# Four raw weight buffers in both expert layers, with the residual input kept outside meanwhile

## The reference

```python
x = x + merged @ w_out[l]
h2 = rmsnorm(x, norm2_g[l])
x = x + peer(h2, ...)           # below
return rmsnorm(x, final_g)
...
# peer, for each token and each of 8 heads: 16 experts out of 128 x 128
s1, s2 = scores of the two halves of the query against 128 keys each
v1, i1 = lax.top_k(s1, PEER_TOPK); v2, i2 = lax.top_k(s2, PEER_TOPK)
vals, flat = lax.top_k(v1 + v2 over all pairs, PEER_TOPK)
gates = jax.nn.softmax(vals, axis=-1)
hid = jax.nn.gelu(jnp.einsum('cd,chkd->chk', xc, u_tab[ec]))
return jnp.einsum('chk,chkd->cd', gc * hid, v_tab[ec])
```

## Time and profile before

| | us |
|---|---|
| runs | 2459.35, 2459.76, 2462.13 |
| median | 2459.76 |
| the profiled execution, its time | 2455.19 |
| its span, first to last instruction | 2453.5 |
| mean granted TensorE clock | 0.988 |
| first unit of the first expert layer starts | 962.8 |
| first unit of the second expert layer starts | 1725.5 |

### The profile page before, as it was taken

One profiled execution on the slowest core, in us unless ns is written; L12 is line 12 of the kernel. 1 busy time (PEld: TensorE's weight loads), 2 busy tenths in 40 slices (PEclk: granted clock), 3 DMA queues, 4 the chain that ended last, 5 costly groups with the idle time before them and its releaser, 6 DMA issues.

```text
span 2453.5 us, 33787 instructions
## 1 busy us (share of the span) xinstructions
PE 2359.6 (96%) x12326; PEld 2047.5 (83%) x12326; DVE 1642.7 (67%) x2048; ACT 1168.2 (48%) x1072; POOL 516.4 (21%) x348
## 2 busy tenths in 40 slices
PE   7999999999999999989989999999999999999997
PEld 6888888888878889988878899999788888888885
DVE  5545766555645555898898888784577666667674
ACT  5534555444444344565556455564443334333342
POOL 0012322000000001222222546453221021211210
PEclk9999999999999999999999999999999999999998
DMA  7755556444466545555555678777898787887871
GB/s 281 267 198 202 215 204 220 151 148 168 141 240 221 217 187 188 194 206 210 210 184 207 255 295 300 286 290 257 338 360 313 267 313 298 306 306 309 317 273 74
DMA packets 91231, 589.99 MB, mean 240 GB/s; under 512 B 10912, under 2 KB 11168, under 8 KB 28944
## 3 DMA queue, kind: packets, MB, share of 16 engines
q1 hardware_dynamic: 58464, 423.65, 47.2%
q0 software_dynamic: 21744, 123.09, 13.6%
q10 hardware_dynamic: 10944, 42.18, 4.3%
HBM read 543.79 MB, written 44.04 MB: 240 GB/s over the span
## 4 chain that ended last, share of the span: by engine, by line
PE 65%; DVE 16%; DMA 9%; issue 6%; ACT 4%; DVEq 0%; SPq 0%; ACTq 0%; POOL 0%; POOLq 0%
PE psum L1196 10%; PE psum L1198 9%; PE psum L1197 9%; PE psum L840 9%; PE psum L842 9%; PE psum L841 9%; DMA w_raw<-in_w_units 8%; DVE w_lo L1250 6%; ACT w_hi L487 3%; DVE hot2a L1596 3%; DVE hot1a L1592 1%; PE psum L974 1%; PE psum L1146 1%; DVE pre_ring L1639 1%; PE psum L1099 1%
## 5 line engine op out<-in xcount | busy, mean ns | idle before, releaser
L1250 DVE TENSOR_TENSOR w_lo<-w_raw,w_hi 128x2048 fp32r<-128x2048 f32 x276 | 637.7, 2317 | 338.9 <-ACT w_hi L487 334.8
L487 ACT ACTIVATE w_hi<-w_raw 128x2048 fp32r<-128x2048 f32 x276 | 527.8, 1914 | 574.8 <-DMA w_raw<-in_w_units 527.6
L1146 PE MATMUL psum<-h2T,w_hi 128*128 128x448 f32 x2048 | 648.8, 375 | 25.7 <-DVE w_lo L1250 16.9
L1147 PE MATMUL psum<-h2T,w_lo 128*128 128x224 f32 x2048 | 544.0, 266 | 0.0
L1146 PEld LDWEIGHTS psum<-h2T,w_hi 128*128 128x128 f32 x2048 | 384.6, 188 | 60.8 <-issue 29.1
L1196 PE MATMUL psum<-w_hi,w_up 128*128 128x512 f32 x1024 | 401.5, 392 | 9.7 <-ACT hs L769 5.2
L1197 PE MATMUL psum<-w_lo,w_up 128*128 128x512 f32 x1024 | 400.3, 391 | 0.0
L1198 PE MATMUL psum<-w_hi,w_low 128*128 128x512 f32 x1024 | 400.3, 391 | 0.0
L1147 PEld LDWEIGHTS psum<-h2T,w_lo 128*128 128x128 f32 x2048 | 391.0, 191 | 0.0
L840 PE MATMUL psum<-w_hi,hT_hi 128*128 128x512 f32 x768 | 306.2, 399 | 12.5 <-DVE w_lo L1250 12.5
L842 PE MATMUL psum<-w_hi,hT_lo 128*128 128x512 f32 x768 | 300.5, 391 | 0.0
(11 more groups left out here) (325 smaller groups left out, 2897.3 us busy)
## 6 DMA issues: line engine op xcount, KB each, us to landing
w_raw<-in_w_units SPq DMA_DIRECT2D x338, 1024.0 KB, 4.9
raw_x<-in_w_units SPq DMA_DIRECT2D x62, 1024.0 KB, 7.6
hid_scratch<-hst ACTq DMA_DIRECT2D x32, 448.0 KB, 2.8
tab_scratch<-gate_a ACTq DMA_DIRECT2D x14, 1024.0 KB, 5.3
h_in<-hid_scratch POOLq DMA_DIRECT2D x16, 896.0 KB, 9.3
g_tab<-tab_scratch POOLq DMA_DIRECT2D x16, 896.0 KB, 14.4
proj_scratch<-evac ACTq DMA_DIRECT2D x24, 512.0 KB, 5.2
x_nat<-in_x POOLq DMA_DIRECT2D x2, 2048.0 KB, 8.7
```

The costliest lines, as they stand in the source:

```text
L487: act.activation(w_hi[:, s % SPLIT, :], w_raw[:, s % RAW, :], ACT.Copy).then_inc(hi_done, 1)
L1146: pe.matmul(psum[:, k % 4, 0:2 * NU].rearrange("p (a t) -> p a t", a=2), uh, h2T[:, c, :, G:S], start=c == 0, stop=False, skip_group_check ...
L1147: ins = pe.matmul(psum[:, k % 4, NU:2 * NU], ul, h2T[:, c, 0, G:S], start=False, stop=c == KC - 1, skip_group_check=True)
L1250: dve.tensor_tensor(w_lo[:, s % SPLIT, :], w_raw[:, s % RAW, :], w_hi[:, s % SPLIT, :].bitcast(F32), ALU.subtract).then_inc(lo_done, 1)
```

## The change

From unit U0 on there are four raw buffers: the two of `w_raw` and two of `raw_x`, which now lie in the place of `x_nat`. For that x leaves the core. POOL writes `x_nat` to a DRAM scratch `x1` as soon as its last block is added, `x_rep` is filled from there, and POOL reads it back into a new tile `x_end` (in the former place of `raw_x`) in the second layer, when the last hidden store has landed. The end of the kernel works on `x_end`. In the second layer the gathered rows are used at other steps: none at k = 1 and 3 of iteration 0, one each at k = 5 and 7, then k = 1, 3 and 5 as before, with the step (5, 1) left out instead of (4, 5).

```diff
-        region(AT_MIX + 16 * KB, AT_MIX + 32 * KB, ("raw_x", [P, 2, UW]))
+        region(AT_X, END, ("raw_x", [P, 2, UW]))
+        region(AT_MIX + 16 * KB, AT_MIX + 32 * KB, ("x_end", [P, NT, D]))
...
-            with sp.Fori(1, (V0 + XR) // RAW) as i:
+            with sp.Fori(1, U0 // RAW) as i:
...
-                sp.wait_ge(hi_done, V0 + XR + s - RAW + 1)
-                sp.wait_ge(lo_done, V0 + XR + s - RAW + 1)
-                sp.dma_start(w_raw[:, s, :], io["w_units"][V0 + XR + s]).then_inc(w_in_s[s], 16)
-            sp.wait_ge(hid_st[0], 16 * U_IT)
-            sp.wait_ge(hid_st[1], 16 * U_IT)
-            sp.wait_ge(gidx_done, 1)
+                sp.wait_ge(hi_done, U0 + s - RAW + 1)
+                sp.wait_ge(lo_done, U0 + s - RAW + 1)
+                sp.dma_start(w_raw[:, s, :], io["w_units"][U0 + s]).then_inc(w_in_s[s], 16)
+            sp.wait_ge(x1_spilled, 16)
+            sp.wait_ge(sq2, 8)
+            sp.wait_ge(xg2_done, 4)
             for s in range(2):
-                sp.dma_start(raw_x[:, s, :], io["w_units"][V0 + XR + 2 + s]).then_inc(w_in_x[s], 16)
-            with sp.Fori(1, (PEER_NK - XR) // XR) as i:
+                sp.dma_start(raw_x[:, s, :], io["w_units"][U0 + 2 + s]).then_inc(w_in_x[s], 16)
+            with sp.Fori(1, (UNITS - U0) // XR) as i:
                 for s in range(XR):
-                    sp.wait_ge(hi_done, i * XR + (V0 + s + 1))
-                    sp.wait_ge(lo_done, i * XR + (V0 + s + 1))
+                    sp.wait_ge(hi_done, i * XR + (U0 + s - XR + 1))
+                    sp.wait_ge(lo_done, i * XR + (U0 + s - XR + 1))
...
+            pool.wait_ge(x1_done, 4)
+            pool.dma_start(x1, x_nat[:, :, :]).then_inc(x1_spilled, 16)
             pool.wait_ge(xt_done, 4)
...
-            pool.wait_ge(x1_done, 4)
+            pool.wait_ge(x1_spilled, 16)
             pool.wait_ge(sc_done, 2)
...
-                pool.dma_start(x_rep[g * G:(g + 1) * G, :], x_nat[0:G, 0, :]).then_inc(rep_in, 16)
+                pool.dma_start(x_rep[g * G:(g + 1) * G, :], x1[0:G, 0, :]).then_inc(rep_in, 16)
...
+            pool.wait_ge(hid_st[0], 16 * U_IT)
+            pool.wait_ge(hid_st[1], 16 * U_IT)
+            pool.wait_ge(gidx_done, 1)
+            pool.dma_start(x_end[:, :, :], x1).then_inc(x1_back, 16)
...
-                    m = 3 * i + k // 2
-                    if k in (1, 3, 5) and m != GJ - PRE:
-                        n = PRE + m - (m > GJ - PRE)
-                        if n < 2 * GJ:
-                            gathered(n)
+                    if (i, k) in row_slots:
+                        gathered(row_slots[i, k])
...
+            open_slots = [(0, 5), (0, 7)] + [(i, k) for i in range(1, U_IT) for k in (1, 3, 5) if (i, k) != (5, 1)]
+            row_slots = dict(zip(open_slots, range(PRE, 2 * GJ)))
...
+            dve.wait_ge(x1_back, 16)
```

More of the change, by code:

```diff
@@ L180, in hybrid_block @@
         x_rep, y_acc, ring, pre_ring, raw_x = buf["x_rep"], buf["y_acc"], buf["ring"], buf["pre_ring"], buf["raw_x"]
+        x_end = buf["x_end"]
         sel = buf["rs_diag"][:, 0, :]
@@ L481, in hi @@
             def hi(n, s):
+                if isinstance(n, int) and n >= U0:
+                    return hi_wide(n, s)
                 act.wait_ge(w_in_s[s % RAW], (n - s % RAW) * (16 // RAW) + 16)
@@ L487, in hi, with hi_wide @@
                 act.activation(w_hi[:, s % SPLIT, :], w_raw[:, s % RAW, :], ACT.Copy).then_inc(hi_done, 1)
-            def hi_second(i, s):
-                if isinstance(i, int) and i == 0 and s < XR:
-                    return hi(V0 + s, s)
-                slot, turn = s % XR, i * 2 + (s // XR - 1)
+            def hi_wide(n, s):
+                slot = s % XR
                 if slot < 2:
-                    act.wait_ge(w_in_s[slot], turn * 16 + 16 * ((V0 + XR) // RAW + 1))
-                else:
-                    act.wait_ge(w_in_x[slot - 2], turn * 16 + 16)
-                act.wait_ge(unit_done, i * 8 + (V0 + s - (SPLIT - 1)))
-                src = w_raw[:, slot, :] if slot < 2 else raw_x[:, slot - 2, :]
+                    src = w_raw[:, slot, :]
+                    act.wait_ge(w_in_s[slot], (n - (U0 + slot)) * (16 // XR) + 16 * (U0 // RAW + 1))
+                else:
+                    src = raw_x[:, slot - 2, :]
+                    act.wait_ge(w_in_x[slot - 2], (n - (U0 + slot)) * (16 // XR) + 16)
+                act.wait_ge(unit_done, n - (SPLIT - 1))
                 act.activation(w_hi[:, s % SPLIT, :], src, ACT.Copy).then_inc(hi_done, 1)
@@ L817, in _ @@
                 act.wait_ge(x2_done, t + 1)
-                act.activation(sq_last[:, :], x_nat[:, t, :], ACT.Square, accum_out=stat[:, t:t + 1]).then_inc(fsq, 1)
+                act.activation(sq_last[:, :], x_end[:, t, :], ACT.Square, accum_out=stat[:, t:t + 1]).then_inc(fsq, 1)
                 act.wait_ge(fms, t + 1)
@@ L1244, in lo @@
             def lo(n, s):
+                if isinstance(n, int) and n >= U0:
+                    return lo_wide(n, s)
                 dve.wait_ge(hi_done, n + 1)
@@ L1729, in _ @@
             dve.wait_ge(gf_in, 16)
+            dve.wait_ge(x1_back, 16)
             for t in range(NT):
                 dve.wait_ge(acc_done, t + 1)
-                dve.tensor_tensor(x_nat[:, t, :], x_nat[:, t, :], psum[:, 4 * t:4 * t + 4, :].rearrange("p b n -> p (b n)"), ALU.add).then_inc(x2_done, 1)
+                dve.tensor_tensor(x_end[:, t, :], x_end[:, t, :], psum[:, 4 * t:4 * t + 4, :].rearrange("p b n -> p (b n)"), ALU.add).then_inc(x2_done, 1)
                 dve.wait_ge(fsq, t + 1)
@@ L1737, in _ @@
                 step(refine(stat[:, 6 + t:7 + t], stat[:, 2 + t:3 + t], 1))
-                dve.scalar_tensor_tensor(out_t[:, t, :], x_nat[:, t, :], stat[:, 6 + t:7 + t], gf[:, :], ALU.mult, ALU.mult).then_inc(out_done, 1)
+                dve.scalar_tensor_tensor(out_t[:, t, :], x_end[:, t, :], stat[:, 6 + t:7 + t], gf[:, :], ALU.mult, ALU.mult).then_inc(out_done, 1)
 ROUND = float(3 << 22)
```

20 lines of the change are left out of this document (10 added, 10 removed).

## The result

| | before | after |
|---|---|---|
| median us | 2458.15 (10 runs, 2455.97 to 2462.50) | 2465.09 (10 runs, 2460.77 to 2468.91) |
| span of the profiled execution | 2453.5 | 2459.3 |

The ratio is 1.0024 (95% interval 1.0014 to 1.0035): the changed kernel is **slower by 0.24%, some 6 us**, where 20 us less were forecast.

What follows compares the result with a forecast made beforehand. TensorE was taken as the bound, with idle or low-clock losses in four places, and VectorE in the first layer's iterations 0 to 7. Terms: -7.9 - 20.5 - 1.6 - 4.0 + 0.6 + 13 = -20.4 us, giving 2439.4, range 2420 to 2464.

Steps and rivals of the forecast that it cites:

- Part 1: First layer, iterations 0 to 7: four raw buffers remove VectorE's waits for w_hi and nothing else, -7.9 us.
- My last sentence: Forecast wrong if TensorE still waits for hot2a, or something unseen in the waits held VectorE's w_lo in iterations 0 to 7.
- Part 2: First layer, iterations 8 to 13: TensorE becomes the bound, idle and clock losses go, -20.5 us, between -10 and -21.7.
- iterations 14 and 15: End of the first layer: the time that TensorE misses there goes, -1.6 us.
- Part 3: Start of second layer: stall at the hs copy goes, but iteration 1's g_tab lands late; -4.0 us, between -8.3 and 0.
- only iteration 1 inherits the late start: +0.6: Second layer, iterations 1 to 4: same slack as before, so just the first of them loses, 0.6 us.
- Part 4: Second layer, iterations 5 to 14: moved rows delay operand loads, an iteration takes 32.4 + L; +13 us, between 0 and +41.
- L: Second layer: g_tab's time from issue to landing, taken as 12.5 us; under 11.1 an iteration takes 43.5.
- The port rule: Second layer: VectorE would hold every gather at the moved rows 2 us more, making the sum -0.4, not -20.4.
- the first term: First layer, iterations 0 to 7: the -7.9 us for VectorE's waits for w_hi.
- (b): Rival, slower: operand load decides the second layer, 49.0 us an iteration, +55 there; +22 in all, 2481; chance 0.14.

Runs made afterwards that it cites:

- half_raw: The kernel after, with only half of each raw weight unit loaded from the first layer's fifth unit on: 2437.69 us, ratio 0.9904 to the kernel before.
- no_skip: The kernel after, with step 1 of iteration 5 no longer left out of the second layer's gathered rows: 2445.09 us, ratio 0.9935 to the kernel before.
- old_slots: The kernel after, with the second layer's gathered rows back in their old steps throughout: 2436.46 us, ratio 0.9899 to the kernel before.

## Why the prediction was wrong

**Part 1: "all of its waits for w_hi and nothing else goes: -7.9".** This step failed, in two ways. First, the waits for w_hi went, 7.0 us of them inside the stage, but VectorE's idle time fell by 4.2 only, as behind 11 of them w_lo waited 0.25 us each for VectorE's own search. Second and larger, I took VectorE's busy time of 335.1 us as a fixed sum. It was not: ScalarE, which no longer waited 138.7 us for w_raw, copied the second of two products to hs 7 us earlier, and POOL's instructions fell beside s_now and wholly beside the product on hot, no longer beside the cast. VectorE's busy time rose by 7.6 us, and -4.2 + 7.6 is the measured +3.4. The trace of before had the sign: one cast of 128x32 took 1.02 us on average, another of the same shape 0.18. My last sentence (that w_lo might be held by something the waits do not show) was near, but it named w_lo, which took 2.7 us more in all, and not hot, and gave no price.

**Part 2, and iterations 14 and 15.** Right: 47.6 and five times 47.3, a clock of 1.00, TensorE busy all of the 283.80 us. The gain of 21.8 is at the far bound given, 21.7. VectorE's waits for w_hi fell from 53.0 to 12.6 us and not to nothing, behind slack.

**Part 3, the landing for iteration 1.** The mechanism was right (the stall at the hs copy goes, g_tab comes too late), three sizes were off. From the first gather to the landing took 38 us (T+3.9 to T+42.0) and not 35.0: x_end costs 7.3 and not 5.4, and the raw load that I credited with -2.7 gave at most 1.2, as the queue's work without x_end took 31 us against 32.3. Worst was "only iteration 1 inherits the late start: +0.6": iterations 1 and 2 took 5.5 us over 87.0, since the row of step 1 that the next operand load now waits for was itself late by the stall. The old steps took back 4.0 of them.

**Part 4.** The step is right and so is its formula: L plus 32.2 where the clock stays full, at L = 14.0 (after) and 11.8 to 12.8 (half_raw), and L plus 33.2 where it falls; the sum had 32.4. The term was mis-sized by L. (The low clock delays the issue by 1.1 us in four of the ten iterations, and L is about as much shorter there.) I took 12.5 from "1.5 MB less on the same 16 DMA engines, 2 to 4 us if all of it stood ahead; I take half of that". Halving all raw loads brought it to 12.5. At its later place g_tab landed 0.8 us sooner (13.8 for 14.6); what of that is the fewer raw loads was not separated. So the loss was 24.3 and not 13. That is inside the bounds given (0 to 41). Each us of L costs some 10 us, so the sum hung on this number more than the chances said: L = 13.5 to 15 had 0.1.

**The port rule.** By the gather of 3.04 us I feared that the gather at the moved step would be held as well. In iterations 5 to 14 it took 0.93 or 0.94 us: VectorE paused 0.35 us or more for w_hi behind the row (0.88 in iteration 7), and the gather started ahead of w_lo. In iteration 1, with w_lo directly behind the row, it started second and took 2.74. The rule that I looked up (the Trainium skill, "SBUF — State Buffer", "Who interferes with whom") bore on the first term, where I did not apply it: VectorE and GpSimd share a port pair that one instruction holds while the other waits. The runs agree (2.57 against 0.76 us on hot). The same section infers that an operation like w_lo, with two inputs, leaves the descriptors of POOL's DMAs alone. The gather of 2.74 us beside a w_lo does not bear that out; it also reads its row numbers, and no run separates the two.

**Rivals.** Of (b) the mechanism came, at 46.2 and not 49.0 an iteration. No rival had a longer routing stage. The total, 2465, touches the edge of (b) by another way: (b) had +55 in iterations 5 to 14, the runs +24.3, and the rest are parts 1 and 3.

**Open.** Why g_tab takes 16.5 us in no_skip and 14.4 in old_slots with the same steps from iteration 5 on. It is issued at T+20.8 in one and at T+16.9 in the other: in no_skip VectorE never makes up its late start, and reaches the row at step 1 some 4 us later each time. Why the landing takes 2 us more there is not shown. Open too is why g_tab lands at the same T+39.5 to T+39.7 when it is issued 1.1 us later, and why VectorE's busy time in the routing stage differs by up to 3 us between like kernels.

## What to carry to other kernels

When a wait goes from an engine that is off the bound, ask what it issues earlier and beside which instruction of the bound engine that falls, and which wait stands behind the one that goes; look in the trace for one instruction of a shape that takes two or five times what its like takes. When a load is put behind a step of a loop, write the loop's period as constant + landing time, and take the landing time from rows under the traffic of that loop, without a discount that no row shows. A change of several parts is to be judged part by part: here all but the new steps gave -1.0%, the new steps alone +1.1%.
